# The last pair of experts read in 2 MB transfers

## The reference

```python
def moe(h, w_router, b_router, w_gate, b_gate, w_up, b_up, w_down, b_down):
    ...
    top_v, top_i = lax.top_k(logits, TOP_K)
    top_w = jax.nn.softmax(top_v, axis=-1)
    ...
    def expert_block(args):
        xb, e = args
        gate = jnp.minimum(xb @ w_gate[e] + b_gate[e], SWIGLU_LIMIT)
        up = jnp.clip(xb @ w_up[e] + b_up[e], -SWIGLU_LIMIT, SWIGLU_LIMIT)
        act = (up + 1.0) * gate * jax.nn.sigmoid(SWIGLU_ALPHA * gate)
        return act @ w_down[e] + b_down[e]
    ...
x = x + moe(rmsnorm(x, g_ffn), ...)
gate_p = jax.nn.sigmoid(rmsnorm(x, g_ple) @ w_ple_gate)
x = x + gate_p * (p @ w_ple_proj)
```

## Time and profile before

| | us |
|---|---|
| median of 3 runs | 1261.71 (1260.11 to 1261.73) |
| profiled execution, its own time | 1259.79 |
| its span, first to last instruction | 1258.0 |
| TensorE busy | 1205.6 (96%) |
| VectorE busy | 344.4 (27%) |
| ScalarE busy | 171.7 (14%) |
| granted TensorE clock, mean | 0.989 |
| read from HBM | 454.41 MB, 366 GB/s over the span |

### The profile page before, as it was taken

One profiled execution on the slowest core, in us unless ns is written; L12 is line 12 of the kernel. 1 busy time (PEld: TensorE's weight loads), 2 busy tenths in 40 slices (PEclk: granted clock), 3 DMA queues, 4 the chain that ended last, 5 costly groups with the idle time before them and its releaser, 6 DMA issues.

```text
span 1258.0 us, 15770 instructions
## 1 busy us (share of the span) xinstructions
PE 1205.6 (96%) x6478; PEld 621.9 (49%) x6478; DVE 344.4 (27%) x729; ACT 171.7 (14%) x437; POOL 48.6 (4%) x129
## 2 busy tenths in 40 slices
PE   9999999999999999898999999999989898999897
PEld 8857888855434434343454343443434343434344
DVE  3165335533221312211221212130312212121234
ACT  3135304111100001000100110000101000000103
POOL 2211100010000000000000000000000000000002
PEclk9999999999999999999999999999999999999999
DMA  9937812598999999999999999999999999999971
GB/s 341 301 128 254 303 67 67 220 394 317 413 420 430 428 427 428 426 428 429 427 427 427 428 427 429 427 427 429 427 432 427 428 429 427 432 426 422 421 288 37
DMA packets 57383, 461.20 MB, mean 367 GB/s; under 512 B 5712, under 2 KB 6789, under 8 KB 28398
## 3 DMA queue, kind: packets, MB, share of 16 engines
q1 hardware_dynamic: 52096, 445.17, 85.2%
q0 software_dynamic: 3280, 10.75, 2.7%
q10 hardware_dynamic: 1950, 4.44, 1.1%
HBM read 454.41 MB, written 6.39 MB: 366 GB/s over the span
## 4 chain that ended last, share of the span: by engine, by line
PE 72%; DMA 26%; ACT 0%; DVE 0%; issue 0%; SPq 0%; ACTq 0%; POOLq 0%; POOL 0%
PE bank L1180 29%; DMA arena<-in_w_gate_dram 12%; DMA arena<-in_w_up_dram 10%; PE bank L733 9%; PE bank L1218 7%; DMA arena<-in_w_down_dram 4%; PE bank L1270 4%; PE bank L785 3%; PE bank L1082 3%; PE bank L714 2%; PE bank L1317 1%; PE bank L774 1%; PE bank L937 1%; PE bank L961 1%; PE bank L1334 1%; PE bank L1196 1%
## 5 line engine op out<-in xcount | busy, mean ns | idle before, releaser
L1180 PE MATMUL bank<-arena 128*64 128x512 f32 x2352 | 517.3, 595 | 8.8 <-DMA arena<-in_w_up_dram 6.0
L1180 PEld LDWEIGHTS bank<-arena 128*64 128x64 f32 x2352 | 169.8, 137 | 338.3 <-issue 336.2
L1218 PE MATMUL bank<-arena 128*64 128x512 f32 x720 | 169.8, 625 | 30.9 <-DMA arena<-in_w_gate_dram 30.7
L1218 PEld LDWEIGHTS bank<-arena 128*64 128x64 f32 x720 | 57.8, 143 | 130.2 <-issue 130.1
L733 PE MATMUL bank<-arena 128*128 128x264 f32 x512 | 115.9, 387 | 0.0
L2106 DVE TENSOR_TENSOR arena<-bank,arena 128x264 f32<-128x264 f32 x112 | 48.5, 433 | 211.3 <-PE bank L1270 210.3
L733 PEld LDWEIGHTS bank<-arena 128*128 128x128 f32 x512 | 96.6, 190 | 16.8 <-issue 0.2
L2088 DVE COPY arena<-bank 128x512 f32<-128x512 f32 x16 | 11.1, 692 | 222.8 <-PE bank L1180 222.8
L2076 DVE TENSOR_SCALAR arena<-bank 128x512 f32<-128x512 f32 x32 | 20.6, 686 | 179.0 <-PE bank L1180 179.0
L1589 ACT ACTIVATE arena<-arena 128x1024 f32<-128x1024 f32 x16 | 16.9, 1057 | 355.1 <-DVE arena L2066 355.0
L1082 PEld LDWEIGHTS bank<-arena 128*128 128x128 f32 x512 | 58.4, 192 | 13.3 <-issue 13.0
(11 more groups left out here) (269 smaller groups left out, 776.2 us busy)
## 6 DMA issues: line engine op xcount, KB each, us to landing
arena<-in_w_gate_dram SPq DMA_DIRECT2D x52, 2048.0 KB, 24.8
arena<-in_w_up_dram SPq DMA_DIRECT2D x52, 2048.0 KB, 25.0
arena<-in_w_down_dram SPq DMA_DIRECT2D x52, 2048.0 KB, 24.8
arena<-in_w_in_dram SPq DMA_DIRECT2D x13, 2048.0 KB, 11.9
arena<-in_w_gate_dram SPq DMA_DIRECT2D x24, 1024.0 KB, 15.6
arena<-in_w_up_dram SPq DMA_DIRECT2D x24, 1024.0 KB, 16.3
arena<-in_w_down_dram SPq DMA_DIRECT2D x22, 1024.0 KB, 13.3
out_dram<-arena POOLq DMA_DIRECT2D x9, 512.0 KB, 6.3
```

What stands on the lines that cost most here:

```text
L1180: ins = pe.matmul(out[c][hp(one), :], src[:, k * P + CAP * one:k * P + CAP * one + CAP], w[one][:, j, halves(c)], start=(first and k == 0) ...
L1218: ins = pe.matmul(GATE[c][hp(one), :], xT_e[:, k * P + CAP * one:k * P + CAP * one + CAP], w[one][:, j, halves(c)], start=(k == 0), stop=F ...
```

## The change

The gate and up weights of pair 15 and the first half of its down weights are read as twins. The last four singles (numbers 44 to 47 of the 48 of pairs 14 and 15: down's quarters 2 and 3 of both experts) stay as they were, with the last two in halves. TensorE's waits and its counting of used places follow.

```diff
+        SINGLE = 2 * NGRAN * PER - 4
-        last_loads = [sum(a % RING == g for a in range(2 * NGRAN, 2 * NGRAN * PER)) for g in range(RING)]
+        last_loads = [sum(a % RING == g for a in range(SINGLE, 2 * NGRAN * PER)) for g in range(RING)]
...
-            load_twins(PAIRS - PER, NE - 2 * PER, NGRAN)
-            load_experts(PAIRS - PER, NE - 2 * PER, range(2 * NGRAN, 2 * NGRAN * PER - 2))
+            load_twins(PAIRS - PER, NE - 2 * PER, SINGLE // 2)
+            load_experts(PAIRS - PER, NE - 2 * PER, range(SINGLE, SINGLE + 2))
...
-                        if twins:
+                        if twins and not (last and at_ >= SINGLE):
...
+                        single = not twins or (last and m == 2 and g >= 2)
...
-                                    if j == 1 and c == 1 and not (g == 3 and one == 1) and (g % 2 or not twins):
-                                        ins.then_inc(s_used, n_used)
+                                    if j == 1 and c == 1 and not (g == 3 and one == 1) and (g % 2 or single):
+                                        ins.then_inc(s_used, 1 if single else 2)
...
-            pair(PAIRS - PER, 0, twins=True)
-            pair(PAIRS - PER, 1, last=True)
+            pair(PAIRS - PER, 0, twins=True, next_twins=True)
+            pair(PAIRS - PER, 1, last=True, twins=True)
```

More of the change, by code:

```diff
@@ L1135, in granules @@
                         elif isinstance(i0, int):
-                            pe.wait_ge(s_gr[at_ % RING], 16 * (first_loads[at_ % RING] + (at_ - 2 * NGRAN) // RING + 1))
+                            pe.wait_ge(s_gr[at_ % RING], 16 * (first_loads[at_ % RING] + (at_ - SINGLE) // RING + 1))
                             yield gran[at_ % RING]
```

## The result

| | before | changed |
|---|---|---|
| median of 5 runs, us | 1261.71 (1260.11 to 1264.94) | 1267.0 (1265.91 to 1270.31) |
| profiled execution, us | 1259.79 | 1265.91 |
| its span, us | 1258.0 | 1264.1 |

The ratio is 1.0044, with a 95% interval of 1.0026 to 1.0061: slower by about 0.44%, 5.3 us in the medians. I had forecast slower by 2.8 us, 1264.5, with a range up to 1266.4. The direction is right, the size is short by half, and the time is outside the range.

What follows compares the result with a forecast made beforehand. Up's last landing in pair 15 was taken to set the end. Added work behind it, + 3.43, less 0.66 for faster transfers, gave + 2.8 us: from the median 1261.71 to 1264.5, slower by 0.22%, range 1262.0 to 1266.4.

Steps and rivals of the forecast that it cites:

- What bounds the kernel: Last weight transfers of pair 15: the last landing of up sets the end, and no wait on DMA is left behind it.
- Step 2: Up of pair 15: steps 2 and 3 both wait for the last landing, 7.02 us instead of 3.59, adding 3.43 us.
- Step 1: Gate and up transfers of pair 15: 428 instead of 421 GB/s lands up 0.66 us earlier, 1.56 as the other bound.
- Step 3: TensorE at gate of pair 15: some 4.5 us of lateness is behind the wait for up and costs nothing.
- Step 4: Down of pair 15: its twins land at 1198.6, before the down steps start at about 1200.3; costs nothing.
- Step 5: SyncE's issues: ten fewer, some issued later, but still with transfers queued in front; costs nothing.
- A: Last down products: lower clock doesn't come back, saving up to 1.4 us; 1263.1, not slower, chance 0.14.
- B: Weight transfers: larger ones save a fixed cost, TensorE's 3.5 us of DMA waits in pair 15 go; 1258.2, faster, chance 0.04.
- C: Pair 15's transfers: the slowest engine gains as well, sum + 1.9 us; 1263.6, within 0.2%, chance 0.14.
- D: Gate step 2 of pair 15: lower clock after a longer wait adds 0.6 us, 3.4 in all; 1265.1, slower, chance 0.10.

Runs made afterwards that it cites:

- the kernel with 118: Kernel before plus 118 increments of an unused semaphore on SyncE behind the last weight loads; median 1263.34 us, ratio 1.001.
- changed once more: The changed kernel unaltered, profiled and run again beside the kernel before; median 1266.71 us of 9 runs, ratio 1.0047.
- padded by ten: Changed kernel plus ten increments of an unused semaphore on SyncE, restoring its old program length; median 1264.65 us, ratio 1.0021 to the kernel before.
- by five: Changed kernel plus five increments of an unused semaphore on SyncE behind the last weight loads; single run 1268.76 us.
- the profile with nine: Changed kernel plus nine increments of an unused semaphore on SyncE behind the last weight loads; single run 1263.56 us.

## Why the prediction was right or wrong

*What bounds the kernel: right.* Up's last landing set the end, and the rows of pair 15 came within 0.6 us of the forecast.

*Step 2, what is left behind that landing: right.* From landing to the next instruction were 1196.29 - 1189.14 = 7.15 us, forecast 7.02 + 0.14; before, 3.72. This is the 3.4 us.

*Step 1, the pace: mis-sized.* I took 0.66 us off for the higher rate. The rate did rise: over 1148.8 to 1189.1 us the trace of the changed kernel has 428 GB/s, where before it is 421:

```profile
1148.80:1189.10 40.30, 35.05 (x155) 13.68 (x155) 7.22 (x13) 5.21 (x11) 0.00 (x0) 0.96 1.01 428
```

But the landing that counts came only 0.3 us earlier, and over more profiles not at all. From pair 14's last down wait to the matmuls behind up's last landing were 40.7 us before, 39.7 in both the kernel with 118 and the one with down's twins alone (all of up and gate in singles), and 39.9 to 40.4 in the four with both as twins (changed, changed once more, padded by ten and by five). Two instruction fetches fall into that stretch in each. The mean rate counts all sixteen engines, a landing the last one. That the fetches hold up the slowest engine more when packets are larger would fit; it was not tried. The price on the path is therefore 2.6 to 3.1 us against the profile of before, and 3.6 to 4.1 against the other two. That my + 2.8 came so close to the 3.0 of the medians is in part luck: the 0.66 us were not gained at the landing, and the landing that I started from, 1189.45, was 1 us later than in the other two profiles with singles. The spread of 1.6 us that the range allowed for the runs was that of three; 35 runs of the kernel before spread over 8.3.

*Step 3, a late gate costs nothing: right in this kernel, wrong as a reason.* It was hidden by up's own lateness. Alone it costs 1 to 2 us. *Step 4, down costs nothing: the same.* Alone it costs 3.0 us in the medians. The three parts, priced one by one by their medians, come to 2.1 (gate, in part the low clock), 3.0 (up) and 3.0 (down). Together they cost 3.0, not 8, since they lie in each other's shadow.

*Step 5, SyncE, is the step that failed.* I wrote "It has ten issues fewer" and "Cost nothing", and in the first part "What comes behind runs as it did". The instructions behind did stay the same, but their place in SyncE's program did not. The paddings of 10, 9, 5 and 118 instructions show in both directions that 2.3 us hang on this place: a step of 2.7 to 2.8 us in four profiles and of 0.5 us in eight. This step, taken at nothing, is what put the time outside the range; with it padded away the changed kernel ran at 1264.65, against 1264.5 forecast. The sum with the true sizes: 3.0 (the median of the kernel padded by ten over the kernel before) + 2.3 = 5.3 us, which is what was measured.

*The rivals.* A: the low clock at the last down products came back in the changed kernel, as in ten of the other eleven profiles. (The shorter wait for up that A counted on, 0.6 to 1.1 us, was 1.54.) The profile with nine had it not, and shows its price:

```profile
1198.32 0.59 PE L1208 MATMUL bank<-arena 128*128 128x128 f32 x3
...
1202.21 13.95 PE L1185 MATMUL bank<-arena 128*64 128x512 f32 x64
1216.10 3.83 PE L1275 MATMUL bank<-arena 128*128 128x264 f32 x16
```

From the end of up to the mix it took 17.78 us, the changed kernel 19.33: 1.55 us, where I had put up to 1.4. B, the transfers gaining far more, is out: 428 GB/s, as the twins had. The Trainium skill (DMA: Bandwidth & Descriptors, section Anatomy of one DMA — SWDGE (gpsimd) path) fits a transfer issued from GpSimd with a fixed part of about 2.0 us. The trace of the changed kernel does not show it for this full queue fed by SyncE: eight transfers fewer brought the landing 0.3 us forward, not the 16 us estimated from that fit. C gave back nothing. D was seen at gate step 2 in the kernel with gate alone (1.65 us) and not in the changed one. There the clock fell one piece earlier (granted 0.64 from 1159 to 1163, the 8.51 us above), and TensorE still waited 1.29 us for the next twin, which hid it.

## What to carry to other kernels

A larger transfer makes its consumer wait for all of it. At the end of a stream, where no other work stands behind, keep the pieces small, and price a larger one by the work that now waits for the last landing, against the rate it gains. Here pieces smaller than 1 MB for up gained nothing that the runs could measure. Price each part also by itself: a delay that costs nothing may only be hidden by the other delay of the same change. And where a change alters the number of instructions on an engine whose last jump ends the program, compare the last wait and the drain in both profiles before explaining a few us by the work.

## What the runs showed that I had not expected

- SyncE's step from its last wait over the unused second pass to its drain takes 0.5 us or 2.7 to 2.8 us, by its place. One instruction fetch of 8192 bytes is made between that wait and the drain in all four slow cases and in none of the eight fast ones. Four instructions more or less decide it.
- A wait on a transfer is often paid twice: the granted clock falls to its lower level (1.2 instead of 2.4 GHz) for a part of the work behind it. After 3.64 us of waiting 32 matmuls took 9.66 instead of 7.09 us; after 2.72 us 16 took 5.30 instead of 3.65; after 2.31 us, and 1.81 ahead of it, 64 took 16.84 instead of 13.95. It does not always happen: in the kernel padded by ten, gate step 2 also waited 2.72 us and took 3.65, and in the trace of before two of the four such waits of 2.68 to 2.70 us were followed by the full clock.
- The profiles reach pair 14's last landing up to 8.7 us apart (1148.7 before, 1157.5 with 118), though TensorE's and SyncE's programs are the same up to there, and the two of the changed kernel 3.3 us. The runs of before spread from 1259.2 to 1267.5 us, so distances within a profile, from one common landing, tell more than 12 runs do. But they too vary by 1 us between profiles with the same transfers, and a price under that is not shown by one of them.
